# Request order of the experts' weights, order of the last products, and matmuls of constants, in a two-block transformer kernel

## The reference

```python
x = x + hybrid_mixer(rms_norm(x, norm_mix_g[l]), ...)
x = x + cross_attention(rms_norm(x, norm_x_g[l]), ...)
x = x + hierarchical_moe(rms_norm(x, norm_ffn_g[l]), ...)   # 4 groups x 8 experts, top 2 in the best group
...
def run_block(args):                                         # one expert's rows
    x_blk, e = args
    return (jax.nn.silu(x_blk @ w1[e]) * (x_blk @ w3[e])) @ w2[e]
...
x = x + short_conv_mixer(x, ln_a[i], w_in_a[i], conv_a[i], w_out_a[i])
x = x + swa_sink_mixer(...)
```

## Time and profile before

| | us |
|---|---|
| Median of 3 runs | 1531.57 |
| Lowest and highest | 1528.35, 1532.67 |
| The profiled execution, its time | 1528.55 |
| The profiled execution, its span | 1526.7 |
| TensorE busy in the span | 1342.1 |
| Mean granted clock | 0.944 |

### The profile page before, as it was taken

The page is one execution under the profiler, slowest core; times in us unless marked ns, Lnnn a source line. Parts: engine busy times, 40 slices in busy tenths (PEclk is TensorE's granted clock), DMA queues, the critical chain, the costliest instruction groups (busy, mean ns, idle before and its releaser), DMA issues. The chain is left out here.

```text
span 1526.7 us, 16626 instructions
## 1 busy us (share of the span) xinstructions
PE 1342.1 (88%) x6268; PEld 889.6 (58%) x6268; DVE 536.8 (35%) x1068; ACT 413.8 (27%) x803; POOL 392.9 (26%) x372
## 2 busy tenths in 40 slices
PE   7999996999899579888888888865999998998798
PEld 6777764898658523332222223225888887886466
DVE  3659747330052512111111111127411326473552
ACT  5333454164331100000000000024222224444441
POOL 7553242167500011111111111100435530000220
PEclk9999988999999689999999999997999999999899
DMA  7211212154204849999999999973323222322000
GB/s 204 94 73 56 106 60 83 42 177 141 83 5 193 358 185 421 423 421 424 420 423 422 423 423 421 423 297 128 111 83 111 83 83 83 111 83 83 8 15 35
DMA packets 72369, 298.27 MB, mean 195 GB/s; under 512 B 10169, under 2 KB 10217, under 8 KB 51569
## 3 DMA queue, kind: packets, MB, share of 16 engines
q1 hardware_dynamic: 64848, 282.80, 47.1%
q0 software_dynamic: 7456, 14.59, 3.0%
HBM read 293.16 MB, written 12.58 MB: 200 GB/s over the span
## 5 line engine op out<-in xcount | busy, mean ns | idle before, releaser
L740 POOL TENSOR_TENSOR ring_rounded<-ring,ring_rounded 128x512 fp32r<-128x512 f32 x192 | 255.0, 1365 | 324.7 <-ACT ring_rounded L1435 324.6
L862 PE MATMUL bank<-HT_rounded,ring_rounded 128*128 128x512 f32 (+1 forms) x576 | 222.1, 386 | 5.4 <-DVE ring_rounded L2292 4.5
L863 PE MATMUL bank<-ring_rounded 128*128 128x512 f32 (+1 forms) x576 | 218.6, 379 | 0.0
L864 PE MATMUL bank<-HT_rounded,ring_rounded 128*128 128x512 f32 (+1 forms) x576 | 218.4, 379 | 0.0
L1155 PE MATMUL bank<-ring,B 128*64 128x512 f32 x704 | 180.1, 664 | 42.9 <-DMA ring<-in_w 42.0
L1155 PEld LDWEIGHTS bank<-ring,B 128*64 128x64 f32 x704 | 55.0, 151 | 151.6 <-issue 113.7
L2184 DVE TENSOR_TENSOR B<-bank,small 128x512 f32<-128x512 f32 x32 | 22.1, 691 | 331.2 <-PE bank L1145 331.2
L864 PE MATMUL bank<-ring_rounded 128*128 128x512 f32 x352 | 138.6, 394 | 0.0
L1435 ACT ACTIVATE ring_rounded<-ring 128x2048 fp32r<-128x2048 f32 x56 | 106.4, 1915 | 109.9 <-DMA ring<-in_w_in_a 47.8
L862 PEld LDWEIGHTS bank<-HT_rounded,ring_rounded 128*128 128x128 f32 x576 | 109.3, 190 | 32.4 <-issue 9.4
L863 PEld LDWEIGHTS bank<-ring_rounded 128*128 128x128 f32 x576 | 109.4, 190 | 20.5 <-issue 1.0
(11 more groups left out here) (375 smaller groups left out, 1964.1 us busy)
## 6 DMA issues: line engine op xcount, KB each, us to landing
ring<-in_w SPq DMA_DIRECT2D x88, 1024.0 KB, 30.3
A<-in_w SPq DMA_DIRECT2D x21, 2048.0 KB, 28.7
ring<-in_w SPq DMA_DIRECT2D x11, 2048.0 KB, 28.8
XN<-in_w SPq DMA_DIRECT2D x20, 1024.0 KB, 29.1
HT<-in_w SPq DMA_DIRECT2D x20, 1024.0 KB, 32.3
ring<-in_w_in_a SPq DMA_DIRECT2D x16, 1024.0 KB, 5.1
ring<-in_w_in SPq DMA_DIRECT2D x14, 1024.0 KB, 7.2
ring<-in_w_in_b SPq DMA_DIRECT2D x8, 1024.0 KB, 5.4
```

Source lines behind the costliest of these rows:

```text
L740: last = pool.tensor_tensor(r32(lo), lo, r32_read(quarter(g, True)[:, k, :]), ALU.subtract)
L862: pe.matmul(o, r32(a_hi), r32(b_hi), start=first, stop=False)
L863: pe.matmul(o, r32(a_hi), r32(b_lo), start=False, stop=False)
L864: return pe.matmul(o, r32(a_lo), r32(b_hi), start=False, stop=last)
```

## The change

Three things are changed. SP requests experts 3 and 4 in another order: first the four halves of w1 and w3 of both, then the two w2. TensorE does the down product of expert 30 before the hidden product of expert 31 instead of behind it. And a helper `spin(o, n)` issues n matmuls of constants (identity by 256 columns of the constant table) into a bank that the next real product overwrites; it is called at five places: 5 before the rank counts, 12 before the table, 8 before the first expert's rows are turned, 9 before the first rows of the second block are turned, once `x3_ready` is there, and 4 before the first product of c0.

```diff
-            def load_expert(e, slot):
-
-                for n, (dst, src, loaded) in enumerate(expert_pieces(e, slot)):
+            def load_expert(e, slot, which=range(5)):
+
+                pieces = list(expert_pieces(e, slot))
+                for n in which:
+                    dst, src, loaded = pieces[n]
                     sp.wait_ge((half_done, half_done, h_done, h_done, y_done)[n], e - 2)
                     sp.dma_start(dst, src).then_inc(loaded, 16)
...
-            load_expert(3, 0)
-            load_expert(4, 1)
+            for which in (range(4), range(4, 5)):
+                load_expert(3, 0, which)
+                load_expert(4, 1, which)
...
+            def spin(o, n):
+
+                for _ in range(n):
+                    pe.matmul(o[:, 0:2 * P], ident, cst[:, 0:2 * P], start=True, stop=True)
...
             o = fill(U, "rank")
+            spin(o, 5)
             pe.wait_ge(sem("chosen_ready"), 1)
...
             o = fill(U, "table")
+            spin(o, 12)
             pe.wait_ge(sem("onehots_ready"), 1)
...
-                if not isinstance(e, int) or e > 0:
+                if not isinstance(e, int) or 0 < e < EXPERTS - 1:
                     step_down(i, n - 1)
...
+            spin(bank[0], 8)
             step_turn(0, 0)
...
-            for n in range(2, 8):
+            for n in range(2, 7):
                 step(4, n)
+            step_down(4, 6)
+            step(4, 7)
             step_down(4, 7)
...
             def turn_x4(t):
 
-                pe.wait_ge(sem("x4n_ready"), t + 1)
                 for b in range(2):
                     o = fill(V, "x4_t", t, b)
+                    if t == 0 and b == 0:
+                        pe.wait_ge(sem("x3_ready"), 1)
+                        spin(o, 9)
+                    pe.wait_ge(sem("x4n_ready"), t + 1)
...
             part = chunk("c0")
+            spin(outs[0], 4)
```

## The result

| | before | after |
|---|---|---|
| Median of four runs, us | 1530.43 | 1521.51 |
| Lowest and highest | 1528.35, 1532.67 | 1520.2, 1523.04 |
| Ratio, with its 95% interval | | 0.9943 (0.9925 to 0.996) |
| The profiled execution, its time and span | 1528.55, 1526.7 | 1522.8, 1521.0 |
| Mean granted clock | 0.944 | 0.956 |

The change takes off 8.9 us, or 0.57%. The forecast was 1523.0 in a range of 1516.5 to 1529.5; against the median of 1531.57 that it started from, that is 8.6 us.

What follows compares the result with a forecast made beforehand. Weight DMA was taken to pace the expert stage, TensorE the end from 1050 us. 3.5 + 3.2 + 0.8 + 0.1 = 7.6 us off 1528.55 gave 1520.9, put 2 us up to 1523; range 1516.5 to 1529.5.

Steps and rivals of the forecast that it cites:

- (1) Request order: Weight requests after the first experts: 7.0 us of DMA idleness become about 3.7, gaining 3.5 us (2.5 to 3.8).
- the idleness only moves: Weight requests: expert 4's down weights start when they did, the order gives 0, total 1526.5 us; 10 in 100.
- (2) Constants in the route: Route to first expert: constant matmuls in TensorE's waits raise the clock, saving 3.2 us together.
- The counts: Rank counts: five constants before them raise the clock 6 times in 10, saving 1.4 us, on average 0.85.
- The table: Table behind twelve constants: 4.10 us cold, 2.05 warm; saves 0 to 2.05 us, on average 1.2.
- The eight: Before the first expert's turn: save 1.66 us on the expert and 0.35 on the turn; 1.2 net (-1.5 to +2.0).
- waits of 1.4 us should hold it: TensorE's remaining waits: the clock should survive 1.4 us, and mostly not 2 to 3 us.
- (3) The tail: Before c0: nine and four constants keep c0 from starting cold, 1.7 us at 45 in 100, so 0.8 us.
- (4) The last products' order: Last two experts: expert 30's down product before expert 31's hidden one brings the gate 0.1 us earlier.
- the clock holds everywhere: All places with constants: clock terms give 7.2 us, with the order 10.8, total 1519.8 us; 8 in 100.
- constants don't raise the clock: All constant groups: they stand cold ahead of ready work, +4.3 us, less 3.5 is +0.8; 5 in 100.
- the clock holds nowhere: Waits left after constants: the clock does not hold, only the order's 3.5 us remain, total 1527 us; 15 in 100.

Runs made afterwards that it cites:

- expert 5's halves: Changed kernel with expert 5's four w1 and w3 halves also requested ahead of expert 4's w2: 1518.57 us, ratio 0.9927.
- the best kernel: Changed kernel plus expert 5's early requests, six constants before the counts, eighteen before the table, three in the last gate's wait: 1518.36 us, ratio 0.9918.
- the requests alone: Kernel before with only the new request order, expert 5's early requests included; no constants, old order of last products: 1521.53 us, ratio 0.9953.

## Why the prediction was right, and where its terms were not

**(1) Request order: right in its mechanism, sized too small.** 3.5 us were predicted; the stretch that it governs shrinks by 4.1 to 4.3 us in three profiles (428.16 alone, 428.01 and 428.07 in the changed kernel). The working took the idleness left as about 3.7 us, from 574 to 577.8 us (which is 3.8); the row from 574.5 to 577.9 shows 2.5, since the data ran on to 574.5 us and the share between was not nothing but 0.26. That the second down product's wait takes over is what the request at 577.24 shows, and expert 5's halves, which fill that wait with data, confirm it. The rival that the idleness only moves is out: 7 us of it became 2.5.

**(2) Constants in the route: right on the whole, wrong in how the groups stand to each other.** 3.2 us were predicted. The profile after shows 3.6; over the seven profiles with five, twelve and eight constants it is 2.2 on average (49.56 us against 51.77 in the four without any), from 0.5 to 3.7.
- The counts are at full clock in four of the nine profiles with five constants ahead of them; 6 in 10 was said. The ten records themselves are cold throughout in all nine (4.61 us), so the rise came later than the 3.4 us that the text went by.
- The table: the step "where they start warm they end 3 us early, and the clock can be lost again" is what happens. In all three profiles with twelve in which the counts are warm, the table is cold (3.79, 4.13, 4.13 us; the wait ahead of it is 3.26 and 3.27 us in the two shown). In the five with the counts cold the twelve take some 7.4 us, leave some 1.0, and the table takes 2.20. The text priced the two savings apart and added them; in these eight profiles with twelve they exclude each other. In the two with eighteen they don't.
- The eight: 1.2 net was taken, on the assumption that expert 0's 1.66 us would go. The 1.66 us go only in the profile after and in the best kernel. In four of the nine profiles with the eight they stay with expert 0 (8.77 to 8.79 us), though the eight were warm and left only 0.81 to 1.00 us ahead of the turn and 0.85 behind it. In three they move to expert 1 (8.78 us in the kernel with constants alone). So "waits of 1.4 us should hold it" does not hold here, and that a loss of clock could move on behind the first expert was not in the working. On the turn the warm eight bring 0.35 us. Where they start cold, behind a cold table, they hold the turn up by about 1.1 us: in the kernel with constants alone and in the one with the old last order, as the text's 0.2 to 1.5 us had it.

**(3) The tail: the size failed at "TensorE sets the end from there".** The clock is up in c0 in five of nine profiles with four constants, about the 45 in 100 that was said, but by luck: across the 1.90 us that the four leave when they run warm it holds in one profile of five. In the other four it had fallen in the transposes before, the four ran partly cold (2.44 to 3.03 us), left only 0.23 to 0.58 us, and it had risen again by then. And a c0 that is warm brings 0.9 us and not 1.7: TensorE comes to the third tile's transposes before DVE has normalised it and waits 0.41 us for it, in the last row above. So 0.5 us on average for the 0.8, and 0.0 in the profile after.

**(4) The last products' order: two errors that cancel.** The gate was costed at 2.3 us, by expert 0, where DVE had other work ahead of it; here it is 1.50, and the last hidden product ends 0.3 us sooner than reckoned. So the gate turns 1.2 us earlier and not 0.1. But behind a gate with nothing in front of it the down product runs at half clock in six of seven profiles: 1.7 us back, 0.5 us lost net. "It trades 3.6 us of product for 2.3 us of gate" left the clock out, although the same text priced a 2.11 us wait at 1.5 us of lost clock. Timed alone the order gives 1.0005, so nothing, as was forecast.

**The rivals.** That the clock holds everywhere is out: it falls behind waits of 1.50 + 0.47, of 1.90 and of 3.26 us. The Trainium skill (TensorE: Matmul & The Clock Gate, Why this matters for your kernels) warns of idle gaps of more than about 3 us between matmul bursts: the fall behind 3.26 us agrees with that, those behind the shorter waits do not. That constants don't raise the clock is out: in the profile after the ten records of the first group take 0.46 us each, the 24 of the second 0.22, and the granted clock is 1.00 from 523 to 527 us, where the four kernels without constants have cold counts (2.85 us) and a cold table (4.10 us). That the clock holds nowhere is out, too, though it comes nearest for the eight. The Trainium skill's other rule (TensorE: Matmul & The Clock Gate, Part 4: PE-mode transpose), by which expert 0 would start cold after its turn, is not what the profile after shows: 7.09 us behind the transposes and 0.85 us of waiting. That the clock rises while TensorE does only transposes, as the prediction read from one profile, is seen in three of the four kernels without constants ahead of c0. In the one with the last products' order alone it stays at 0.50 through the transposes and the first 4.7 us of c0 (from 1043.0 to 1047.0 and from 1047.5 to 1057.0 us).

**The sum.** By the twelve runs: 4.2 + 2.2 + 0.5 - 0.5 = 6.4 us; the two measurements of the changed kernel gave 8.9 and 7.2, with intervals of 2 to 3 us to either side. The forecast, 7.6, lies between them. That it comes so near is in part luck: the first term was 0.7 us too small, the other three together 1.9 too large, and 8.9 and 7.2 are both above the sum of what the profiles show. The profile after gives 9.4 because two clocks that are a matter of chance fell well there (expert 0 and the last down product).

**What stays open.** Why the clock holds behind 1.50 + 0.47 us once and falls six times, with the same instructions ahead. And the 26.9 to 30.0 us from the last down product to c0, which vary from profile to profile for every kernel (in the kernel with the request order alone DVE waits 2.23 us for the second tile's read-back, in the profiles before and after 0.60 and 0.22): 0.6 us of the profile's 9.4 are from there, and no part of the change is known to make them. Nor does a run leave out the five, the twelve, the nine or the four alone, so their shares of the 0.25% are read from profiles and not timed.

## What to carry to other kernels

Where one queue issues transfers in order, sort them by when their waits clear, and look again for the hole that is left: here that gave 4.2 us, then 2 to 3.6 more, in every profile, and the requests alone (0.9953) did as much as the whole change. Matmuls of constants can pay only if they reach up to the data that is waited for and not beyond it. Even then nothing is sure: the table was warm behind 0.68 to 1.07 us of waiting in all seven profiles that have it, but expert 0 was cold in four of the seven profiles with warm constants ahead of its turn, behind 0.81 to 1.00 us, four transposes and 0.85 us. A clock kept at one place is often lost at the next, so they must be judged by the whole stretch, by timed runs and by more than one profile. Before an instruction's cover is moved away, cost the clock behind the bare wait as well as the wait.

## What the runs showed of the hardware

- The same program at the same place is granted one clock in one execution and the other in the next: the last down product 3.65 and 5.35 us, expert 0's hidden product 7.09 and 8.78 us, c0 at 0.51 in one profile and at 1.00 in the other.
- A pair of small waits is enough: 1.50 us, four small records (0.66 us) and 0.47 us ahead of a dense product cost it 1.7 us in six of seven profiles, while 1.49 us with a dense product just before did not in the profile before. Nor is that rule firm: ahead of expert 31's hidden product 1.51 us kept the clock in the profile before, and the same 1.51 us lost it in the kernel with expert 5's requests alone (0.50 from 998.2 to 1001.5 us).
- Sixteen small float32 records of 36 columns, the route's fourth product, keep TensorE busy for 3.60 us and leave it at half clock: the ten records of constants behind it start cold (4.61 us).
- In the tail the wait between the nine constants and the first transposes sorts the ten profiles with constants. With 0.83 to 1.53 us the transposes were warm in all five, with 1.91 to 2.64 us the clock fell just before or in the second tile's eight transposes, behind a further wait of 1.04 us, in all five.
